# Decode read-out of retention in four column tiles, and attention products of two key heads side by side

## The reference

```python
# retention, decode: 8 sequences b, 4 heads, state S (256 x 512) of its own for each b and head
o = intra + (q * q_dec) @ S          # q: 4 tokens x 256
o = o * rsqrt(mean(o * o) + EPS)
# attention, prompt: 8 blocks of 128 queries, 4 key heads of 64 features, 4 query heads per key head
s = q @ kk.T * 64 ** -0.5            # 128 queries x 256 keys (the block before and its own)
p = exp(s - m) / (sum + exp(sink - m))
o = p @ vv                           # 128 x 256 by 256 x 64
```

## Time and profile before

| | us |
|---|---|
| median of three runs | 3052.37 |
| the three runs | 3050.44 to 3052.54 |
| span of the profiled execution, first to last instruction | 3050.0 |
| PE busy | 2976.0 (98%) |
| DVE busy | 1262.6 (41%) |
| ACT busy | 742.6 (24%) |
| POOL busy | 163.7 (5%) |

### The profile page before, as it was taken

How to read it: one execution, slowest core, us unless ns; L and a number is a source line. 1 busy time by engine, 2 the same in 40 slices (tenths; PEclk the granted TensorE clock), 3 DMA queues, 4 the chain that set the end, 5 groups by cost and what they waited for, 6 DMA issues and landing times.

```text
span 3050.0 us, 42635 instructions
## 1 busy us (share of the span) xinstructions
PE 2976.0 (98%) x17496; PEld 2777.9 (91%) x17496; DVE 1262.6 (41%) x1638; ACT 742.6 (24%) x1318; POOL 163.7 (5%) x78
## 2 busy tenths in 40 slices
PE   7999999999999999999999999899899999999999
PEld 7879959968986999999999999689679999999999
DVE  6443443443344633233332355744764233332333
ACT  3131132123123322111222131531553111222111
POOL 2000000000000200000000021211220000000000
PEclk9999999999999999999999999899899999999999
DMA  3122041122213111111111122103001111111111
GB/s 126 64 102 63 29 137 62 45 87 77 64 49 114 42 49 46 45 45 45 45 45 45 45 71 57 45 18 102 19 18 49 46 45 45 45 45 45 45 48 74
DMA packets 91333, 174.50 MB, mean 57 GB/s; under 512 B 9840, under 2 KB 15344, under 8 KB 90416
## 3 DMA queue, kind: packets, MB, share of 16 engines
q1 hardware_dynamic: 89296, 167.40, 17.1%
q10 hardware_dynamic: 1920, 5.41, 0.8%
HBM read 143.83 MB, written 25.56 MB: 56 GB/s over the span
## 4 chain that ended last, share of the span: by engine, by line
PE 92%; DVE 5%; ACT 2%; issue 1%; DMA 0%; ACTq 0%; SPq 0%; DVEq 0%
PE ps L1133 78%; PE ps L1298 2%; PE ps L1275 2%; PE ps L1470 2%; PE ps L1270 2%; PE ps L1444 1%; DVE wlo L701 1%; PE ps L1281 1%; PE ps L1173 1%; PE ps L1457 1%; PE ps L1304 1%; DVE x L738 1%; DVE hlo L708 1%; PE ps L1243 1%; ACT sq L477 1%
## 5 line engine op out<-in xcount | busy, mean ns | idle before, releaser
L1133 PE MATMUL ps<-hhi,whi 128*128 128x352 f32 x2976 | 651.0, 327 | 25.8 <-DVE hlo L708 16.3
L1133 PE MATMUL ps<-hhi,wlo 128*128 128x352 f32 x2976 | 643.5, 324 | 0.0
L1133 PE MATMUL ps<-hlo,whi 128*128 128x352 f32 x2976 | 643.0, 324 | 0.0
L468 ACT CAST whi<-wraw 128x512 fp32r<-128x512 f32 x424 | 261.1, 618 | 1135.2 <-PE ps L1133 1121.7
L701 DVE TENSOR_TENSOR wlo<-wraw,whi 128x512 fp32r<-128x512 f32 x424 | 333.9, 794 | 486.9 <-ACT whi L468 486.9
L1133 PEld LDWEIGHTS ps<-hhi,whi 128*128 128x128 f32 x2976 | 506.9, 190 | 29.7 <-DVE hlo L708 17.8
L1133 PEld LDWEIGHTS ps<-hhi,wlo 128*128 128x128 f32 x2976 | 512.7, 188 | 0.0
L1133 PEld LDWEIGHTS ps<-hlo,whi 128*128 128x128 f32 x2976 | 507.8, 189 | 0.0
L1133 PE MATMUL ps<-ahi,whi 128*128 128x352 f32 x2112 | 460.6, 326 | 9.1 <-DVE alo L1111 6.3
L1133 PE MATMUL ps<-ahi,wlo 128*128 128x352 f32 x2112 | 456.0, 323 | 0.0
L1133 PE MATMUL ps<-alo,whi 128*128 128x352 f32 x2112 | 455.3, 324 | 0.0
(11 more groups left out here) (156 smaller groups left out, 1925.0 us busy)
## 6 DMA issues: line engine op xcount, KB each, us to landing
wraw<-in_weights SPq DMA_DIRECT2D x424, 256.0 KB, 2.6
s<-in_state_in SPq DMA_DIRECT2D x32, 512.0 KB, 3.7
out_state_s<-s SPq DMA_DIRECT2D x32, 512.0 KB, 2.8
zr<-z_a ACTq DMA_DIRECT2D x40, 132.0 KB, 2.4
x<-in_xT SPq DMA_DIRECT2D x8, 528.0 KB, 8.7
rope_tab<-in_tables SPq DMA_DIRECT2D x4, 1056.0 KB, 4.8
out_yT<-x SPq DMA_DIRECT2D x8, 528.0 KB, 2.6
atab<-in_attn_tables SPq DMA_DIRECT2D x2, 1056.0 KB, 5.2
```

What stands on the lines that cost most here:

```text
L468: act.copy(whi[:, i % RING, :], wraw[:, i % RING, :]).then_inc(w_hi, 1)
L1133: mm = pe.matmul(ps[:, 3 * (m % 2) + t, 0:TB], a[:, slot, w], b[:, s * KG + k, t * TB:(t + 1) * TB], start=(first and j == 0), stop=(last ...
```

## The change

In retention the decode read-out is cut into four products of 256 columns per sequence, each into its own 32 partitions of bank 7: (half of the value features) x (half of the key features). DVE then adds the four parts up in `join_sample`, in the unused `k_tok` and `sc_t`, and `norm_o(h, 8)` reads that sum.

In attention the keys are kept once, in `k_a`; a score product uses only the 64 partitions of its head, and the products of the two heads alternate. `block_out` of both heads writes one bank, 64 partitions each. Scores and outputs are now issued per block c (both heads together): PE's loop is `block_scores((k + 3) // 2)` at odd k, `turn_probs(k)`, and `block_out(k // 2 - 1)` at even k. `keep_out` copies 128 partitions once per block. The rest of the diff adapts counts of semaphores.

```diff
-        k_z = at("k_z", o_work + 4 * TT, [P, 2, TOK], F32)
+        k_a = at("k_a", o_work + 4 * TT, [P, TOK], F32)
...
 ACT norm_o
-                bank = 7 if c == CH else 2 + c % 2
-                act.wait_ge(o_done, i + 1)
+                if c == CH:
+                    act.wait_ge(o_sum, 2 * h + 2)
+                    out = o_smp                       # k_tok[0:32], 512 wide
+                else:
+                    act.wait_ge(o_done, i + 1)
+                    out = ps[:, 2 + c % 2, :]
...
 ACT pair, loop
-                    if k >= 2:
-                        keep_out(u - 2, k - 2)
+                    if k >= 3 and k % 2:
+                        keep_out(p, (k - 3) // 2)     # waits pv_done; 128 partitions
...
                     if k >= 2:
-                        act.wait_ge(pv_done, u - 1)
+                        act.wait_ge(pv_done, p * CH + k // 2)
                     act.copy(pt_a[:, u % 2, 1, :], ps[:, 5, :]).then_inc(pt1_kept, 1)
...
 DVE, after the eight steps of a head and before inverse_rms(h, CH)
+            def join_sample(h):
+                dve.wait_ge(o_done, (h + 1) * (CH + 1))
+                dve.tensor_copy(k_tok[0:NS, 0, :], ps[NS:2 * NS, 7, 0:DK])
+                dve.tensor_copy(k_tok[0:NS, 1, :], ps[2 * NS:3 * NS, 7, DK:DV])
+                spare = sc_t[0:NS, :, :].rearrange("p j f -> p (j f)")
+                link(h, dve.tensor_copy(spare, ps[3 * NS:4 * NS, 7, DK:DV]))
+                dve.tensor_tensor(k_tok[0:NS, 0, :], ps[0:NS, 7, 0:DK], k_tok[0:NS, 0, :], ALU.add)
+                link(h, dve.tensor_tensor(k_tok[0:NS, 1, :], ps[0:NS, 7, DK:DV], k_tok[0:NS, 1, :], ALU.add))
+                dve.tensor_tensor(k_tok[0:NS, 1, :], spare, k_tok[0:NS, 1, :], ALU.add)
...
 DVE finish_head: one product over 128 partitions for the keys too; the zeros of k_z (L1063) are gone
 DVE pair, loop
-                        dve.wait_ge(pv_done, u - 1)
+                        dve.wait_ge(pv_done, p * CH + k // 2)
                         dve.tensor_copy(pt_a[:, u % 2, 0, :], ps[:, 4, :]).then_inc(pt0_kept, 1)
...
 PE sample_head
-                for j in range(2):
-                    mm = pe.matmul(ps[0:NS, 7, :], q_sel[:, b % 2, j, :], s0[:, b % S0_RING, j, :], ...)
+                for half in range(2):
+                    for j in range(2):
+                        rows = slice(NS * (2 * half + j), NS * (2 * half + j + 1))
+                        cols = slice(half * DK, (half + 1) * DK)
+                        mm = pe.matmul(ps[rows, 7, cols], q_sel[:, b % 2, j, :], s0[:, b % S0_RING, j, cols], ...)
...
 PE block_scores(p, c)
+                if c:
+                    pe.wait_ge(s_kept, p * HU + 2 * c)
...
                 for r in range(GR):
-                    mm = pe.matmul(ps[:, 2 * s + r // 2, ...], q_a[:, r, c * P:(c + 1) * P], k_z[:, s, keys], ...)
+                    for s in range(2):
+                        half = slice(HD * s, HD * (s + 1))
+                        mm = pe.matmul(ps[:, 2 * s + r // 2, ...], q_a[half, r, c * P:(c + 1) * P], k_a[half, keys], ...)
+                        if r == GR - 1:
+                            mm.then_inc(s_done, 1)
...
 PE block_out(p, c): waits for both units' copies, then
                 for t in range(0 if c else 1, 2):
-                    mm = pe.matmul(ps[:, 6 + s, :], v_a[:, c - 1 + t, :], pt_a[:, u % 2, t, :], ...)
+                    for s in range(2):
+                        half = slice(HD * s, HD * (s + 1))
+                        mm = pe.matmul(ps[half, 6 + c % 2, :], v_a[:, c - 1 + t, half], pt_a[:, s, t, :], ...)
...
 PE sample_scores: one product with k_a in place of two with k_z; turned new keys: two transposes in place of four
 PE pair, loop
-                    if k + 3 < HU:
-                        block_scores(p, k + 3)
+                    if k % 2 and k + 3 < HU:
+                        block_scores(p, (k + 3) // 2)
...
-                    elif k == 3:
-                        block_out(p, 1)
-                        block_out(p, 2)
-                    elif k:
-                        block_out(p, k - 1)
-                block_out(p, HU - 1)
+                    if k and k % 2 == 0:
+                        block_out(p, k // 2 - 1)
+                block_out(p, CH - 1)
```

More of the change, by code:

```diff
@@ L224, in trunk @@
         o_kept = sem("o_kept")
+        o_sum = sem("o_sum")
         ot_done = sem("ot_done")
@@ L524, in norm_o @@
                 act.wait_ge(rr_done, i + 1)
-                act.mul(o_tok[0:rows, :], ps[0:rows, bank, :], stat[0:rows, 3:4]).then_inc(o_kept, 1)
+                act.mul(o_tok[0:rows, :], out, stat[0:rows, 3:4]).then_inc(o_kept, 1)
             def ret_head(h, first, last):
@@ L607, in exponentials, with keep_out @@
                 act.activation(ast[:, st + 8:st + 12], ast[:, st + 8:st + 12], ACT.Exp).then_inc(p_done, 1)
[L609 to L615, removed]
+            def keep_out(p, c):
+                act.wait_ge(pv_done, p * CH + c + 1)
+                act.copy(q_a[:, :, c * P:(c + 1) * P],
+                         ps[:, 6 + c % 2, :].rearrange("p (r t) -> p r t", r=GR)).then_inc(out_kept, 1)
             def pair(p):
@@ L646, in pair @@
                 act.wait_ge(nk_done, p + 1)
[L647 to L650, removed]
+                act.copy(nk[:, 0, :], ps[:, 7, 0:P]).then_inc(nk_kept, 1)
+                act.copy(nk[0:NS, 1, :], ps[0:NS, 7, P:2 * P]).then_inc(nk_kept, 1)
                 exponentials(p * HU, 0)
@@ L880, in ret_head @@
                     update_sample(h, c)
+                join_sample(h)
                 inverse_rms(h, CH)
@@ L980, in finish_head @@
                 dve.wait_ge(spread_done, 3 * tile_use(p, m) + part + 1)
[L981 to L988, removed]
+                head = q_a[:, m, :] if m < GR else k_a
+                dve.tensor_tensor(head[:, tok], z_a[:, m % 2, tok], wide_part(part), ALU.mult).then_inc(zq_done, 1)
             def scale_scores(p, k):
@@ L1412, in sample_scores @@
                     pe.matmul(ps[0:NS, 4 + b // 3, col:col + P], q_bd[:, b, :], kc[:, b, :], start=True, stop=True)
-                    for s in range(2):
-                        mm = pe.matmul(ps[0:NS, 4 + b // 3, col + P:col + KEYS], q_bd[:, b, :], k_z[:, s, SEQ:TOK],
-                                       start=(s == 0), stop=(s == 1))
+                    mm = pe.matmul(ps[0:NS, 4 + b // 3, col + P:col + KEYS], q_bd[:, b, :], k_a[:, SEQ:TOK],
+                                   start=True, stop=True)
                 mm.then_inc(sas_done, 1)
@@ L1443, in block_scores @@
                     col = (r % 2) * 2 * P
-                    mm = pe.matmul(ps[:, 2 * s + r // 2, col + lo:col + 2 * P], q_a[:, r, c * P:(c + 1) * P],
-                                   k_z[:, s, keys], start=True, stop=True)
-                mm.then_inc(s_done, 1)
+                    for s in range(2):
+                        half = slice(HD * s, HD * (s + 1))
+                        mm = pe.matmul(ps[:, 2 * s + r // 2, col + lo:col + 2 * P], q_a[half, r, c * P:(c + 1) * P],
+                                       k_a[half, keys], start=True, stop=True)
+                        if r == GR - 1:
+                            mm.then_inc(s_done, 1)
             def turn_probs(p, k):
```

65 lines of the change are left out of this document (30 added, 35 removed).

## The result

The changed kernel takes 3030.23 us (four runs, 3029.58 to 3031.99), the kernel before beside it 3052.09 (four runs): a ratio of 0.9933, 95% interval 0.992 to 0.9945, or 21.9 us less. The prediction had 3040 and the right sign. The profiled execution's span is 3027.8 us against 3050.0. The two parts pull against each other: by the traces the attention stage starts 28.8 us sooner (the turn of the values at 1878.46 us, 1907.25 before) and takes 6.6 us longer in its two pairs. The stretches of the four heads in retention, from the first state product to the product behind the last read-out, add up to 218.7 us, 249.2 before: 30.6 us less, of which 1.8 us are lost on the way to the attention stage; where, I leave open.

What follows compares the result with a forecast made beforehand. PE, 92% of the chain of waits, was taken as the bound. Retention -20.5 us and attention +8.6 made -11.9, so 3052.4 became 3040 us; range 3018 to 3078, the forecast's own 3031 to 3049.

Steps and rivals of the forecast that it cites:

- four calls then fill five slots: Retention read-out: passes in written order overlap partly, 1.08 us, gaining 0.64 us each, 20.5 us over 32.
- two bounds: Retention read-out: passes one after another 1.73 us, no gain; all four tiles together 0.43 us, a gain of 1.29.
- The cover: Retention step: DVE's 0.94 us idle before L800 hides the 0.64 us gain, so the whole step moves up.
- the rival with all tiles together: Read-outs gain up to 1.29 us, about 1.0 remains: -32; attention about +1 a pair; 3022 us, chance 0.13.
- The decode sum: Retention, four times: `join_sample` adds 2.8 us on VectorE, some 3.0 with waits; 0.7 us of cover left, price nothing.
- The attention loop: Attention: chain of waits through DVE makes 9.30 us per two units against 8.65; three rounds, +2.0 us a pair.
- start: Attention, head of each pair: shorter L987 and earlier scores bring work forward 1.6 to 4.2 us; 3.5 taken.
- end: Attention, from the turn of unit 12: `keep_out` at 16.27 us against 14.01 now, +2.3 us a pair.
- clock: Attention: granted clock falls after two of five gaps of about 3 us, 1.7 us each: +3.5 us a pair.
- No overlap: Rival: tiles never run together; retention 0 to +14, attention +16 a pair; 3084 to 3098 us, chance 0.12.
- uncovered loads: Rival, retention read-out: column tiles share rows, so four first weight loads of 0.109 us stand uncovered; chance 0.13.
- The clock that gives all back: Clock rival, in attention: the clock's loss gives back the gain, attention losing 46 us in all; chance 0.17.

Runs made afterwards that it cites:

- e1: Kernel before with only the retention part of the change (four tiles, joined sample rows), attention as before: 3023.47 us, ratio 0.9915.
- experiments 3 and 4: 3: kernel before with the attention part, read-out cut into four but in one tile: 3062.44 us. 4: changed kernel, read-out in two column tiles: 3032.24 us.
- experiment 5: Changed kernel with VectorE's decode-state update ahead of the same chunk's inverse root mean square, in seven of eight steps of a head: 3022.88 us, ratio 0.9903.
- experiment 6: Changed kernel with 24 transposes that nothing reads in TensorE's gap ahead of turns of even units in the attention loop: 3016.77 us, ratio 0.9891.
- e10: Changed kernel with next block's scores ahead of outputs, third turned-probabilities buffer, ScalarE's block copy behind the exponentials and unit copy: 3000.59 us, ratio 0.9837.

## Why the prediction was right and where it was wrong

The sign, the bound and the attention chain were right. The number came out 9.8 us high: inside 3018 to 3078, but just below the forecast's own range of 3031 to 3049. 7.4 of the 9.8 are retention (-27.9 us in e1, -20.5 forecast). By the prediction's own signs, from read-out to the next product it forecast about 1.2 us and the trace has 0.57; it forecast steps of 7.2 us and the trace has 6.85.

**The term that was mis-sized** is "four calls then fill five slots: 5 x 0.216 = 1.08 us, a gain of 0.64 us". It rested on passes that start in written order, each tile's second pass behind its own first. The runs show 1.72 us divided by the number of tiles (experiments 3 and 4), so two slots and not five: 0.43 us, and a gain of 1.27. The first passes of all four tiles start together, within 0.02 us, and none waits for another tile's second pass. I chose between two bounds by a rule of order that no row showed; the lower bound, as it turned out, was the price. The Trainium skill ("TensorE: Matmul & The Clock Gate", Part 3) had 2.38 times for three tiles; here four give 1.84 / 0.57 = 3.2 times, shape change included. The same part of the Trainium skill has the rule that loads run beside a product in flight only where rows differ; this trace does not agree, as it has all eight loads of a read-out in 0.16 us, four of them beside passes on the same rows.

**The cover.** "DVE's 0.94 us of idle time before L800 hides it, so the whole step moves up" was reckoned for 0.64 us and does not hold for 1.27. What then happens stands in the rival with all tiles together: VectorE late at L800, about 1.0 us a step left. Measured 1.03, and the rest came back in experiment 5. That rival was near on retention (-32 forecast, -27.9 in e1) and wrong on attention, so its 3022 us misses by 8 on the other side. What neither had is the first step of the second to fourth head, which gains 0.05 us and not 1.0: there L800 stands behind a root that ScalarE delivers late. The wait of 1.14 us before the last chunk's turn costs next to nothing, as a wait of the kernel before disappeared in its place.

**The decode sum** was priced at nothing under 0.7 us of cover: right. 2.54 us against 2.8, and no idle time before the turn.

**The attention loop** was right as a chain: 9.30 us forecast, 8.99 at full clock, the difference again in outputs that overlap fully (1.87 us and not 2.15). Its price was right for a mixed reason. By the traces, pair by pair:

- start, from the turn of the values to that of unit 6: 51.6 us (59.0 before) and 52.0 us (57.9 before), so -7.4 and -6.0 (forecast -3.5, at most -4.2). In the first pair 4.7 of it stand at the decode probabilities (VectorE's product at 1901.62, 1935.14 before, where the values' turn moved from 1907.25 to 1878.46), near what I had worked out; 2.6 come behind them, where I had put nothing. From the turn of unit 3 to that of unit 6 the kernel before had TensorE at work without a break for 16.4 us; with scores and outputs side by side it is 11.6 us, a gap of 3.11 included. The stretch from the decode probabilities to the turn of unit 3 takes 2.2 us of that back.
- from there to the turn of unit 12: +3.9 and +7.0; from unit 12 to the next weights' product: +5.0 and +4.0. Together +8.9 and +11.0, where loop, end and clock were forecast at +7.8. With the clock held (experiment 6) loop and end are +2.0 in each pair, where +4.3 was forecast; the clock makes the other 6.9 and 9.0 us, where 3.5 was forecast.

Sum +6.6 us, forecast +8.6. In the clock I let two of five gaps fall; the rounds show more falling, and experiment 6, its own cost at the starts included, puts 13.5 us on it. That the sum came near was luck: the clock's loss was priced too low, the chain's loss too high and the start's gain too low, and the misses hid each other.

**Rivals.** No overlap and uncovered loads are excluded by e1 and the rows above. The clock that gives all back did act, with 13.5 us (experiment 6) where that rival's attention loses 46 in all.

## What to carry to other kernels

In this kernel, products that use a part of the array's columns or rows cost nearly their time divided by the number of such tiles side by side (1.72 / n + 0.2 us for the read-out), so price them that way and look at once at the engine next in line: here it ate 0.2 us of 1.27 in most steps, and nearly all of it in three, until one instruction was moved. Pairing work on one engine lengthens the chain through the others; count the round by its waits before its work. Where TensorE has to stand in a loop, the cost here was the stand and then, in most rounds, the half clock behind it, and useless work in the gap (13.5 us) or one more buffer with an order that doesn't hold the next engine (29.6 us, the shorter chain included) gives it back.

## What was not expected of the hardware

- One, two and four column tiles of 32: 1.90, 1.05 and 0.64 us of busy time for the same products in plain fp32, two passes each, with the eight loads of the four tiles in 0.16 us.
- Two row tiles of 64: 16 passes in 1.93 us when neighbours alternate, 2.90 when one tile's eight come first, against 16 x 0.216 = 3.46 in turn (all at a granted clock of 1.00). In the second case passes of the later tile start ahead of passes of the earlier one.
- The granted clock behind like gaps differs: after 3.11 us without work it was 1.00 over the next 5 us in one round and 0.63 over the next 4 in the following, and in e10 after 1.79 us once 1.00 (1936.43) and once 0.67 (behind 1944.15, scores 3.32 us and not 1.93). Behind 1959.93, after 3.11 us without work, it was 0.50 over 5.5 us in which TensorE was busy for 5.47. What decides between them stays open.
